# A two-block transformer kernel: low parts of the gathered rows behind the router's choices, and a re-ordered start of the second block

## What is computed

```python
def rms_norm(x, gain):
    xf = x.astype(jnp.float32)
    y = xf * lax.rsqrt(jnp.mean(xf * xf, axis=-1, keepdims=True) + EPS)
    return (y * gain.astype(jnp.float32)).astype(x.dtype)

def hier_moe(xn, ...):            # 4 groups x 8 experts, D_EXPERT = 512
    g_logits = xt @ w_gr + b_gr   # best group, then the two best experts in it
    ...
    order = jnp.argsort(eid)      # the rows are sorted by expert
    ...
    h = silu(xb @ w_gate[e]) * (xb @ w_up[e]);  out = h @ w_down[e]

def reference(...):
    x = first_block(...)          # ends in h = h + hier_moe(...); rms_norm(h, final_gain)
    return second_block(x, ...)   # begins in proj = rmsnorm(x, norm1_g) @ w_in
```

## Time and profile before

| what | us |
|---|---|
| median of three runs | 1493.04 |
| the profiled execution | 1495.55 |
| its span, first to last instruction | 1493.8 |
| PE busy | 1286.5 |
| DVE busy | 720.6 |
| ACT busy | 528.3 |
| mean granted TensorE clock | 0.950 |

### The profile page before, as it was taken

How to read it: one execution, slowest core, us unless ns; L and a number is a source line. 1 busy time by engine, 2 the same in 40 slices (tenths; PEclk the granted TensorE clock), 3 DMA queues, 4 the chain that set the end, 5 groups by cost and what they waited for, 6 DMA issues and landing times.

```text
span 1493.8 us, 15434 instructions
## 1 busy us (share of the span) xinstructions
PE 1286.5 (86%) x5264; PEld 684.1 (46%) x5264; DVE 720.6 (48%) x1548; ACT 528.3 (35%) x1271; POOL 322.0 (22%) x310
## 2 busy tenths in 40 slices
PE   6987899899989989889999689999977768887776
PEld 6874433333333333388898544544432323333322
DVE  4174110010001000386877676767776766666744
ACT  4432211111111111355663343444534434444433
POOL 6810000000000000000000334443333334433330
PEclk9998999999999999999999899999999899998899
DMA  9563599999999999954325799999999999999995
GB/s 352 185 235 127 226 415 428 428 428 428 428 428 427 428 428 428 348 232 152 112 112 212 313 421 400 417 412 414 419 419 419 421 420 421 419 420 419 421 420 245
DMA packets 64183, 531.32 MB, mean 356 GB/s; under 512 B 12152, under 2 KB 14456, under 8 KB 15736
## 3 DMA queue, kind: packets, MB, share of 16 engines
q0 software_dynamic: 36864, 268.45, 43.6%
q1 hardware_dynamic: 27256, 262.09, 43.4%
HBM read 529.47 MB, written 1.97 MB: 356 GB/s over the span
## 4 chain that ended last, share of the span: by engine, by line
PE 54%; DMA 28%; DVE 11%; ACT 4%; issue 2%; another core or an unknown queue 1%; SPq 0%; POOL 0%; POOLq 0%; ACTq 0%; DVEq 0%
PE bank L1820 17%; DMA ring<-in_w_up 14%; DMA held<-in_uv,row_of 13%; PE bank L1562 11%; PE bank L741 7%; PE bank L1781 3%; PE bank L742 3%; PE bank L1496 3%; DVE held L2388 2%; PE bank L1401 2%; PE bank L1765 1%; PE bank L1586 1%; PE bank L1696 1%; DVE ti L2345 1%; PE bank L1677 1%
## 5 line engine op out<-in xcount | busy, mean ns | idle before, releaser
L1820 PE MATMUL bank<-held,diags 128*128 128x512 f32 x1024 | 485.1, 628 | 116.3 <-ACT diags L1281 116.3
L2388 DVE SCALAR_TENSOR_TENSOR held<-held,bank 128x1024 f32<-128x1024 f32 x256 | 306.3, 1219 | 194.6 <-DMA held<-in_uv,row_of 193.5
L1820 PEld LDWEIGHTS bank<-held,diags 128*128 128x128 f32 x1024 | 198.5, 200 | 399.2 <-issue 216.0
L960 POOL DMA_INDIRECT held<-in_uv,row_of x256 | 241.7, 944 | 636.2 <-PE bank L1820 383.0
L1562 PE MATMUL bank<-ring,x_blk 128*64 128x512 f32 x1024 | 238.6, 620 | 26.9 <-DMA ring<-in_w_up 24.5
L2096 DVE TENSOR_TENSOR hid<-bank,hid 64x512 f32<-64x512 f32 x32 | 22.2, 694 | 413.1 <-ACT hid L1099 413.1
L1562 PEld LDWEIGHTS bank<-ring,x_blk 128*64 128x64 f32 x1024 | 77.7, 142 | 172.9 <-issue 172.6
L1276 ACT ACTIVATE gelus<-dots 128x1 f32<-128x1 f32 x256 | 51.0, 199 | 233.0 <-DVE held L2388 231.9
L1099 ACT ACTIVATE hid<-bank 64x512 f32<-64x512 f32 x32 | 18.8, 588 | 297.1 <-PE bank L1562 297.1
L1281 ACT ACTIVATE diags<-const,hidden 128x128 f32<-128x128 f32 x256 | 102.7, 401 | 52.5 <-PE bank L1820 45.6
L1496 PE MATMUL bank<-ring,hT 128*64 128x512 f32 x512 | 115.6, 592 | 1.2 <-ACT hT L1103 1.2
(11 more groups left out here) (356 smaller groups left out, 1297.5 us busy)
## 6 DMA issues: line engine op xcount, KB each, us to landing
ring<-in_w_gate SPq DMA_DIRECT2D x32, 2048.0 KB, 15.6
ring<-in_w_up SPq DMA_DIRECT2D x32, 2048.0 KB, 19.9
ring<-in_w_down SPq DMA_DIRECT2D x32, 2048.0 KB, 21.9
ring<-in_w_in SPq DMA_DIRECT2D x14, 2048.0 KB, 10.4
ring<-in_w_out SPq DMA_DIRECT2D x4, 2048.0 KB, 8.1
ring<-in_w_q SPq DMA_DIRECT2D x4, 2048.0 KB, 8.0
held<-in_uv,row_of POOLq DMA_INDIRECT x256, 17.4
rel_bias<-rpb_wide SPq DMA_DIRECT2D x4, 512.0 KB, 11.9
```

The source lines that it names most:

```text
L960: pool.indirect_dma_start(held[b][:, :], None, dram["uv"], bass.IndirectOffsetOnAxis(ap=row_of[:, i:i + 1], axis=0)).then_inc(row_full[b], 16)
L1820: last = pe.matmul(bank[SUM_BANK[t] + half][:, :], diags[i % DIAGS][:, :], held[i % ROWS_HELD][:, D + half * 512:D + (half + 1) * 512], st ...
L2388: dve.scalar_tensor_tensor(held[b][:, 0:D], held[b][:, 0:D], 1.0, two_banks[X_BANKS[t]][:, :], ALU.mult, ALU.mult, accum_out=dots[:, i:i + ...
```

## The change

There are seven edits. (1) In `gather` all products with `xhat_lead` come first, then all with `xhat_rest`, and only these wait for `xhat_rest_ready`. (2) DVE takes `xhat_rest` of tile 0 behind `assigned`, and that of tile 1, the weights `wt`, `most_i` and `starts_i` behind `pick_half(0)`. (3) PE loads `most_i` ahead of the `diag` products. (4) The table load for the square root moves on ACT from ahead of `raw_lead(0)` to behind the first square. (5) On DVE `raw_rest` goes ahead of `with_gain`. (6) A new tile `x_turn` is `xhat` times both row factors at once, and PE turns it; h is written later. (7) Leads 16 and 17 move ahead of the `qk` copies on ACT, `rest_half(3)` and `rest_half(4)` move up on DVE, and `window_bias` goes behind `rest_half(7)` and `rest_half(8)`.

```diff
+        x_turn = acts("x_turn", [P, NT, D], 68)
...
-        def pe_turn(pe, m):
+        def pe_turn(pe, m, rows_in_turn):
...
 (ACT)
             act_half(act, SPLIT_IN2 + 0, 1)
-            act.wait_ge(stat_root, 2)
-            act.activation(stat_warm[:, :], stat_sd[:, :], ACT.Sqrt)
...
                 if t == 0:
+                    act.activation(stat_warm[:, :], ident[:, 0:NT], ACT.Sqrt)
                     raw_lead(1)
...
             act_half(act, SPLIT_IN2 + 1, 1)
+            act_half(act, SPLIT_IN2 + 2, 0)
             act_nT_lead(act, 2, "gain12", nT_hi)
+            act_half(act, SPLIT_IN2 + 2, 1)
             act.wait_ge(scale_ready, 1)
...
-            act_half(act, SPLIT_IN2 + 2, 0)
             act.wait_ge(p2_done, 3)
...
             last.then_inc(p2_act, 1)
-            act_half(act, SPLIT_IN2 + 2, 1)
             act.wait_ge(qk_ms, 1)
...
 (PE)
             def gather(part):
                 pe.wait_ge(pick_ready, NT * (part + 1))
-                for k in range(KD):
-                    dst = bank[GATHER_BANK[part][k // 2]][:, (k % 2) * T:(k % 2 + 1) * T]
-                    for rows_of in (xhat_lead, xhat_rest):
+                for rows_of in (xhat_lead, xhat_rest):
+                    pe.wait_ge(*((xhat_lead_ready, NT) if rows_of is xhat_lead else (xhat_rest_ready, NT)))
+                    for k in range(KD):
+                        dst = bank[GATHER_BANK[part][k // 2]][:, (k % 2) * T:(k % 2 + 1) * T]
...
-                    if k % 2:
-                        last.then_inc(gather_done, 1)
-
-            pe.wait_ge(xhat_rest_ready, NT)
+                        if k % 2 and rows_of is xhat_rest:
+                            last.then_inc(gather_done, 1)
+
             gather(0)
+            pe.wait_ge(starts_ready, 1)
+            load_most = pe.value_load(most_i[0:1, 0:1], min_val=0, max_val=T)
             pe.wait_ge(diag_built, 1)
...
-            pe_turn(pe, 2)
+            pe_turn(pe, 2, x_turn)
...
 (DVE)
-            dve.wait_ge(xhat_ready, 2 * NT)
-            slot_rest(0)
             dve.wait_ge(router_done, 1)
...
-            slot_rest(1)
...
+            dve.wait_ge(xhat_ready, 2 * NT)
+            slot_rest(0)
             dve.wait_ge(rank_done, 1)
...
             pick_half(0)
+            link(dve.tensor_reduce(most[:, :], counts[:, :], AX_X, ALU.max))
+            dve.tensor_copy(most_i[:, :], most[0:1, :])
+            dve.tensor_copy(starts_i[:, :], starts[0:1, :]).then_inc(starts_ready, 1)
+            slot_rest(1)
...
             add_moe(1)
+            raw_rest(0)
+            raw_rest(1)
             dve.wait_ge(h_ready, H_COUNT[2])
             with_gain(0)
-            raw_rest(0)
             with_gain(1)
-            raw_rest(1)
             rest_half(1)
...
-            dve.wait_ge(row_turned, 4)
-            for t in range(NT):
-                dve.tensor_scalar(h[:, t, :], xhat[:, t, :], stat_rs1[:, t:t + 1], None, ALU.mult).then_inc(h_ready, 1)
             dve.wait_ge(stat_root, 4)
...
-            dve.wait_ge(h_ready, H_COUNT[3])
-            dve_xhat(dve)
+            dve.wait_ge(scale_ready, 1)
+            for t in range(NT):
+                dve.tensor_scalar(x_turn[:, t, :], xhat[:, t, :], raw_scale[:, t:t + 1], None, ALU.mult).then_inc(xhat_ready, 1)
             rest_half(2)
+            rest_half(3)
             dve_nT_rest(dve, 2, "gain12", nT_hi)
+            rest_half(4)
+            dve.wait_ge(row_turned, 4)
+            for t in range(NT):
+                dve.tensor_scalar(h[:, t, :], xhat[:, t, :], stat_rs1[:, t:t + 1], None, ALU.mult).then_inc(h_ready, 1)
...
-            dve.wait_ge(bias_in, 16 * KROWS)
-            window_bias(0)
-            rest_half(3)
-            window_bias(1)
-            rest_half(4)
...
             rest_half(7)
+            dve.wait_ge(bias_in, 16 * KROWS)
+            window_bias(0)
             for i in range(2):
...
             rest_half(8)
+            window_bias(1)
             dve.wait_ge(qk_turned, 3)
```

More of the change, by code:

```diff
@@ L658, in pe_turn @@
                         last = pe.transpose(bank[b][:, (k % 2) * T + t * P:(k % 2) * T + (t + 1) * P],
[L659 removed]
+                                            rows_in_turn[:, t, k * P:(k + 1) * P], ident)
                 last.then_inc(xhat_turned, 1)
@@ L1317, in _ @@
             pe.wait_ge(const_in, 32)
-            pe_turn(pe, 0)
+            pe_turn(pe, 0, xhat)
             wait_nT_split(pe, 0)
@@ L1498, in expert_out_both @@
                 return last
-            load_most = pe.value_load(most_i[0:1, 0:1], min_val=0, max_val=T)
             with pe.If(load_most > BLOCK):
@@ L2023, in _ @@
             link(dve.tensor_tensor_scan(starts[:, :], c("ones")[:, 0:N_EXPERTS], counts[:, :], 0.0, ALU.mult, ALU.add))
-            dve.tensor_reduce(most[:, :], counts[:, :], AX_X, ALU.max)
             link(dve.tensor_tensor(starts[:, :], starts[:, :], counts[:, :], ALU.subtract))
-            dve.tensor_copy(most_i[:, :], most[0:1, :])
-            dve.tensor_copy(starts_i[:, :], starts[0:1, :]).then_inc(starts_ready, 1)
             link(dve.tensor_tensor(place_of[:, :, :], rank[:, :, :], spread(starts[:, :].unsqueeze(1), [P, NT, N_EXPERTS]), ALU.add))
@@ L2172, in _ @@
             dve.wait_ge(gained, NT)
+            dve.wait_ge(stat_root, 4)
+            link(dve.reciprocal(stat_rs[:, :], stat_sd[:, :]))
+            dve.tensor_tensor(raw_scale[:, :], stat_rs1[:, :], stat_rs[:, :], ALU.mult).then_inc(scale_ready, 1)
+            dve.wait_ge(scale_ready, 1)
+            for t in range(NT):
+                dve.tensor_scalar(x_turn[:, t, :], xhat[:, t, :], raw_scale[:, t:t + 1], None, ALU.mult).then_inc(xhat_ready, 1)
+            rest_half(2)
+            rest_half(3)
+            dve_nT_rest(dve, 2, "gain12", nT_hi)
+            rest_half(4)
             dve.wait_ge(row_turned, 4)
```

17 lines of the change are left out of this document (5 added, 12 removed).

## The result

The changed kernel takes 1484.71 us (median of six runs, 1482.72 to 1486.26), the kernel before beside it 1494.79 (six runs, 1491.64 to 1500.35). The medians lie 10.1 us apart. The measured ratio, an estimate of its own and not the quotient of these two medians (which is 0.9933), is 0.9923, with a 95% interval of 0.9908 to 0.9939: 11.5 us less, 9 to 14 by the interval. Forecast were 9.0 us and 1484.0. The profiled execution has a span of 1483.4 us, where it was 1493.8, so the pair of traces accounts for 10.4.

A forecast was written before the change was run, and what follows sets the result against it. The final chain was 54% TensorE and 28% DMA, with the weight stream bounding the experts. Gains of 3.0 and 6.0 us sum to 9.0, giving 1486.5 for the profiled execution and 1484.0 for the median, range 1481.3 to 1489.5.

The forecast's parts named there:

- Router to first expert: From router's products to first expert: earlier gather and earlier branch start PE on the experts 3.0 us sooner, bounds 1.85 to 3.7.
- read-ahead of some 18 rows: PE's sequencer before the first expert: reads about 18 rows ahead of the array, so the branch is read at 151.8.
- did no harm: PE's wait before the first expert: the 2.32 us at 158.19 was taken as not lowering the clock.
- the 1.2 us of the low part ahead of `lg`: DVE behind the router's products: with tile 0's low part moved back, their result is read 1.2 us earlier.
- Second block: Start of the second block: earlier raw_hi, clock kept up and reordered rests gain 6.0 us, bounds 3 to 7.
- rests 13, 14 and 17: Second block, PE waiting for DVE: three new small waits of 0.5, 0.6 and 1.1 us.
- half clock in half 16: Second block, behind PE's 4.30 us wait: half 16 lost an estimated 1.0 us, now gained.
- all moves rigidly: Behind the second block: nothing is touched, so everything only shifts earlier.
- The clock falls again: Rival, PE's clock near 627 to 630 us and in the gather: gains only 4.5 and 2.5, 1486.0 us; chance 0.2.
- The table load only moves: Rival, ACT ahead of the second raw_hi: up to 1.4 us enter that chain, 1485.3 us; chance 0.08.
- The queues take it back: Rival, both parts: first gains 1.85, DVE and ACT bound the second with 2 us left, 1489.2 us; chance 0.13.
- the third chunk: Slower rival, second block: lead 16 on ACT waits for these weights and holds nT_hi, half 16 and PE, 1498; chance 0.03.

The follow-up runs named there:

- reg_behind: Changed kernel with PE's register load put back behind the diag products, directly ahead of the branch; 1486.03 us, ratio 0.9938.
- before_again: The kernel before, unchanged, traced a second time; one run of 1497.94 us.
- table_only: Kernel before with only the square root's table load moved behind the first square; 1490.42 us, ratio 0.9972.
- rests_early: Changed kernel with both with_gain between the two raw_rest on DVE, and the rest of half 17 ahead of the qk sums; 1485.08 us, ratio 0.9939.
- branch_ahead: Changed kernel with PE's branch directly behind its register load, the diag products behind the first expert's gate and up products; 1483.75 us, ratio 0.9928.
- both_more: Changed kernel with the edits of rests_early and branch_ahead together; 1484.45 us, ratio 0.9933.

## Why the prediction was right, step by step

**Router to first expert: 3.0 forecast, 3.47 in the pair, 3.4 over all traces.** The steps on DVE held to about 0.1 us: `lg` at 136.21 (136.25 forecast), gather at 145.44 (145.55). The branch came at 151.0 where I had 151.8, since the clock rose earlier within the gather (the upper bound of 3.7 had this) and the gather took 5.9 instead of 6.7 us. The read-ahead of some 18 rows held, and `reg_behind` prices the moved load at the 0.9 us that I had.

What the step missed is the first expert itself. I wrote that the wait of 2.32 us before it "did no harm". It did none in that execution. In three other traces with the order of before, it cost 1.7 us. And one item is smaller than I had it: the 1.2 us of the low part ahead of `lg` are gained only where the router's products run at full clock (3.66 us). In `before_again` and `table_only` they take 5.0 and 5.1, and `lg` follows 0.04 us behind them without any edit. Over all traces of the two orders the first expert comes 2.1 us sooner, not 3.0. Shortfall and unforeseen clock about cancel, so that the first part came out at its number is in part luck.

**Second block: 6.0 forecast, 5.65 in the pair, 5.9 over the traces** (66.8, 66.5 and 67.7 with the order of before, 61.12 with the change). The terms: `raw_hi` 1.16 (1.16), clock up behind it (yes), rests 13, 14 and 17 late by 0.49, 0.38 and 1.14 (0.5, 0.6, 1.1), half 16 at 27.53 us behind the combine instead of 33.54, so 6.0 (6.4 forecast). Half 16 came 0.2 later than I had. The other 0.2 is a misreading: I took 656.51 from the chain of waits, where that row begins with the end of the products before, but half 16 had started at 656.31. I gave 1.0 for half clock in half 16 behind the long wait. By the pair it is 0.8: with no late rest the stretch from half 16 to the scores takes 33.59 - 1.14 = 32.45, and before it took 33.23.

**Behind it "all moves rigidly".** It did: from the scores to the queries 125.5 to 125.7 us in all 14 traces. The sum of the parts, 3.4 + 5.9 = 9.3, lies within the interval of the measurement (9 to 14), near its lower end. The two long stretches bound by DMA vary by 1 to 3 us with no edit in them: from the first reload to the last combine 454.9 to 457.8 us, from the queries to the end 676.9 to 678.6.

**The rivals.** "The clock falls again" did not happen in ten traces with the short wait. Its reason was sound: the stretch of 90 to 100 us shows 1.00 and 0.66 in the same code, and a wait of 2.9 us was followed by either clock. "TensorE: Matmul & The Clock Gate", Part 1, of the Trainium skill says that the point of transition differs from run to run. The traces agree and show more than that: the fall as a whole is there in one execution and absent in another.

"The table load only moves" is out (its price of 1485.3 should read 1485.4, 1.4 us above the forecast). The load stands at 626.65 for 1.28 us, and the next `raw_hi` at 628.66 waits 0.51 us for TensorE, not for the load. "ScalarE: Activation LUTs", What ACT_TABLE_LOAD costs, of the Trainium skill adds a drain to the load. No row shows one: in the changed kernel the load starts at 626.65, right behind the instruction before it, and the next activation starts at 627.95, 0.02 us behind its end.

"The queues take it back" was right about the places (the three waits) and too high in size: 2.0 us, and `rests_early` gets them back. ACT never waited for the third chunk.

The branch took 3329 to 3862 ns in 14 traces, and in twelve of them the first expert started 0.1 to 0.2 us behind its end. `x_blk` decides only in `branch_ahead` and `both_more`, where the branch starts 4.4 and 4.0 us before the first expert. "Advanced Engine Details and Errata", Control Flow Timing, of the Trainium skill has 108 ns for it. The traces don't agree, and had it been so, `x_blk` would have decided everywhere.

## What to carry to other kernels

When an engine's queue is the bound, ask which of its passes nobody waits for yet: moving two of them behind the rests that TensorE waits for gave three quarters of the second part, with no work saved. A branch on TensorE that takes 3.3 to 3.9 us, as here, belongs early in its stream, with its register loaded before: the load behind cost 0.9 us. But look at the clock behind it too: with TensorE idle for 1.96 us or more there, the next expert ran at half clock in six of seven traces. Edits of 1 to 3 us in a kernel whose runs lie up to 11 us apart are judged by stretches between fixed instructions, in several traces of each order.

## What the runs showed that I had not expected

- The last combine to half 16 repeats to 0.01 us (27.52 or 27.53 in five traces), while the end of the router's products moves between 135.2 and 141.2 us through the clock, in code that is the same.
- The idle time before the first expert: 1.35 to 1.87 us was followed by full clock in seven of seven traces, 1.96 to 2.70 by half clock in six of seven. What else decides it the traces don't tell.
- A wait of ACT of 3.9 to 5.5 us behind finished products, with no releaser in the trace, shows in 2 of 14 traces, and at most 1.7 us of it are left at the end (678.6 us against the shortest of the others, 676.9). What it is stays open.
